# First norm through a diagonal product, early warm-up on a constant tile, and the first two chunks in pieces

## The reference

```python
def rms_norm(x, g):
    y = x * lax.rsqrt(jnp.mean(x * x, axis=-1, keepdims=True) + EPS)
    return y * g

h = rms_norm(x, norm1_g)
proj = h @ w_in          # split into the recurrent part, q, six k/v parts, gates, merge gates
...                      # recurrent unit, sparse attention, w_out, norm2, convolved FFN
...                      # second block: attention and gated MLP, layer norms, FFN
```

## Time and profile before

| what | value |
|---|---|
| median of 3 runs | 885.41 us |
| all runs | 885.78, 883.08, 885.41 us |
| time of the profiled execution | 883.73 us |
| its span in the trace | 882.0 us |
| mean granted TensorE clock | 0.994 |

### The profile page before, as it was taken

How to read it: one execution, slowest core, us unless ns; L and a number is a source line. 1 busy time by engine, 2 the same in 40 slices (tenths; PEclk the granted TensorE clock), 3 DMA queues, 4 the chain that set the end, 5 groups by cost and what they waited for, 6 DMA issues and landing times.

```text
span 882.0 us, 12692 instructions
## 1 busy us (share of the span) xinstructions
PE 853.0 (97%) x5239; PEld 745.5 (85%) x5239; DVE 576.9 (65%) x733; ACT 488.0 (55%) x713; POOL 37.6 (4%) x44
## 2 busy tenths in 40 slices
PE   6999999999999999999999999999989999999995
PEld 5899999888899998788888888877868788888884
DVE  4672487776765766598877777765765564555555
ACT  4463368777765544476656655435654554554542
POOL 0100200000000000100000000022110000000001
PEclk9999999999999999999999999999999999999999
DMA  6545524132334567245565555575325456456441
GB/s 251 187 145 206 189 84 171 46 138 93 118 132 144 177 229 265 94 171 189 188 199 184 191 192 190 172 239 186 107 74 216 137 189 231 149 187 222 160 143 48
DMA packets 22073, 146.31 MB, mean 166 GB/s; under 512 B 2432, under 2 KB 2688, under 8 KB 7552
## 3 DMA queue, kind: packets, MB, share of 16 engines
q1 hardware_dynamic: 20880, 140.27, 45.5%
q10 hardware_dynamic: 1136, 5.24, 1.7%
HBM read 144.45 MB, written 1.05 MB: 165 GB/s over the span
## 4 chain that ended last, share of the span: by engine, by line
PE 82%; DVE 7%; ACT 4%; issue 3%; DMA 2%; POOL 1%; ACTq 0%; SPq 0%; DVEq 0%; POOLq 0%
PE PS L1454 18%; PE PS L1455 9%; PE PS L1442 8%; PE PS L1444 7%; PE PS L1443 7%; PE PS L1464 7%; PE PS L1466 7%; PE PS L1465 7%; PE PS L1689 2%; DVE WL L897 2%; PE PS L1490 1%; DMA RAW<-in_w_stream 1%; PE PS L1546 1%; ACT WH L546 1%; DVE CG L1287 1%
## 5 line engine op out<-in xcount | busy, mean ns | idle before, releaser
L897 DVE TENSOR_TENSOR WL<-RAW,WH 128x2048 fp32r<-128x2048 f32 (+3 forms) x130 | 287.9, 2216 | 77.7 <-ACT WH L546 77.5
L546 ACT ACTIVATE WH<-RAW 128x2048 fp32r<-128x2048 f32 (+3 forms) x130 | 241.1, 1856 | 81.3 <-PE PS L1466 31.7
L1454 PE MATMUL PS<-CHL,WH 128*128 128x512 f32 x384 | 135.5, 397 | 0.5 <-DVE WL L897 0.3
L1454 PE MATMUL PS<-BHL,WH 128*128 128x512 f32 x352 | 125.4, 400 | 0.1
L1442 PE MATMUL PS<-BHL,WH 128*128 128x256 f32 (+2 forms) x424 | 120.4, 284 | 0.0
L1444 PE MATMUL PS<-BHL,WL 128*128 128x256 f32 (+2 forms) x424 | 119.5, 282 | 0.0
L1443 PE MATMUL PS<-BHL,WH 128*128 128x256 f32 (+2 forms) x424 | 119.5, 282 | 0.0
L1455 PE MATMUL PS<-CHL,WL 128*128 128x256 f32 x384 | 107.7, 281 | 0.0
L1276 DVE TENSOR_TENSOR HLS<-PS,HLS 128x512 f32<-128x512 f32 x46 | 31.8, 692 | 105.1 <-ACT HLS L819 104.3
L1455 PE MATMUL PS<-BHL,WL 128*128 128x256 f32 x352 | 99.0, 281 | 0.0
L1454 PEld LDWEIGHTS PS<-CHL,WH 128*128 128x128 f32 x384 | 72.1, 188 | 18.5 <-DVE WL L897 0.7
(11 more groups left out here) (266 smaller groups left out, 1420.4 us busy)
## 6 DMA issues: line engine op xcount, KB each, us to landing
RAW<-in_w_stream SPq DMA_DIRECT2D x109, 1024.0 KB, 4.9
RAW<-in_w_stream SPq DMA_DIRECT2D x12, 896.0 KB, 5.2
RAW<-in_w_stream SPq DMA_DIRECT2D x8, 768.0 KB, 4.2
WF<-in_w_stream SPq DMA_DIRECT2D x4, 784.0 KB, 4.3
WF<-in_w_stream SPq DMA_DIRECT2D x2, 1024.0 KB, 4.9
LN<-in_ln ACTq DMA_DIRECT2D x2, 1024.0 KB, 6.3
X<-in_x SPq DMA_DIRECT2D x2, 512.0 KB, 4.1
X<-in_x ACTq DMA_DIRECT2D x1, 1024.0 KB, 4.8
```

Source lines behind the costliest of these rows:

```text
L546: eng.activation(WH[:, c % NSLOT, 0:CHUNKS[c][2]], raw(c), ACT.Copy).then_inc(w_hi, 1)
L897: eng.tensor_tensor(WL[:, c % NSLOT, 0:CHUNKS[c][2]], raw(c), f32(WH[:, c % NSLOT, 0:CHUNKS[c][2]]), ALU.subtract).then_inc(w_lo, 1)
L1454: eng.matmul(PS[:, bank, :], wh, HL[:, k, :, :].rearrange("p a t -> p (a t)"), start=(k == 0), stop=False)
```

## The change

The first norm is no longer done on x. DVE multiplies the identity by the inverse roots of a tile, which gives a diagonal DG (128 x 128). TensorE multiplies x (stationary) by DG (moving): that transposes x and scales each token in one ordinary float32 product. The gains are now a column per channel group (G1, 128 x 8) and are applied when PSUM is read: ACT as the scale of its copy (`gained_hi`), DVE in a scalar_tensor_tensor (`gained_lo`), 256 columns at a time.

TensorE first multiplies a tile of ones by itself, 14 times 128 columns wide, written by a memset of DVE. The 8 products with the identity are gone.

The loads G1 and the identity part of CN are issued by ACT. The rest of CN and CV are issued by SP behind chunk 1. ACT's copies of identity and mask move to the first cmp chunk (chunk 4).

Chunk 0 is split in two halves on ACT and DVE, each followed by a pair of channel groups; chunk 1 is split whole, then pairs 2 and 3 follow. TensorE works chunks 0 and 1 by pairs of channel groups (two groups, both tiles), each as soon as it is ready, in place of tile by tile.

Some semaphores are merged: G2R counts on `x_again`, and LN1, OGR and GLN on `rows_in`, of which every reader waits for all three. The numbers computed are those of the reference.

```diff
@@ SP
-            eng.dma_start(G1R[:, :], A_g1.partition_broadcast(P)).then_inc(g1_in, 16)
-            eng.dma_start(CN[:, :], A_consts).then_inc(const_in, 16)
             for c in LOAD_ORDER:
-                if c == 1:
+                if c == 2:
+                    eng.dma_start(CN[:, P:NCONST], A_consts[:, P:NCONST]).then_inc(const_in, 16)
                     eng.dma_start(CV[:, :], A_cols).then_inc(col_in, 16)
@@ ACT
+            def gained_hi(kp):
+                eng.wait_ge(xt_done, kp + 1)
+                for k in (2 * kp, 2 * kp + 1):
+                    last = eng.activation(BH[:, k, :], PS[:, kp, 256 * (k % 2):256 * (k % 2) + TOK], ACT.Copy,
+                                          scale=G1[:, k:k + 1])
+                last.then_inc(xt_hi, 1)
+
+            eng.dma_start(G1[:, :], A_g1).then_inc(g1_in, 16)
+            eng.dma_start(CN[:, 0:P], A_consts[:, 0:P]).then_inc(g1_in, 16)
             for t in range(NT):
                 eng.wait_ge(x_in[t], 16)
                 eng.activation(XN[:, t, :], X0[:, t, :], ACT.Square, accum_out=ssx[:, t:t + 1]).then_inc(x_sq, 1)
-            evict_hi(BH, XT_BANKS[0], xt_done, xt_hi, kps=(0, 1))
-            split(0)
-            evict_hi(BH, XT_BANKS[0], xt_done, xt_hi, kps=(2, 3), first=2)
+            eng.wait_ge(g1_in, 32)
+            eng.wait_ge(raw_in[ARRIVAL[0][0]], 16)
+            for kp, ready in enumerate((w0_half, w_hi)):
+                part = slice(CHUNK // 2 * kp, CHUNK // 2 * kp + CHUNK // 2)
+                eng.activation(WH[:, 0, part], raw(0)[:, part], ACT.Copy).then_inc(ready, 1)
+                gained_hi(kp)
             split(1)
-            eng.wait_ge(const_in, 16)
-            eng.activation(IDR[:, :], ident, ACT.Copy)
-            eng.activation(MASKR[:, :], const("mask"), ACT.Copy).then_inc(masks_ready, 1)
+            gained_hi(2)
+            gained_hi(3)
             for c in range(NCH):
+                if c == AT["cmp", 0]:
+                    eng.wait_ge(const_in, 16)
+                    eng.activation(IDR[:, :], ident, ACT.Copy)
+                    eng.activation(MASKR[:, :], const("mask"), ACT.Copy).then_inc(masks_ready, 1)
@@ DVE
-            eng.wait_ge(g1_in, 16)
+            def gained_lo(kp):
+                eng.wait_ge(xt_hi, kp + 1)
+                for k in (2 * kp, 2 * kp + 1):
+                    last = eng.scalar_tensor_tensor(BL[:, k, :], PS[:, kp, 256 * (k % 2):256 * (k % 2) + TOK], G1[:, k:k + 1],
+                                                    f32(BH[:, k, :]), ALU.mult, ALU.subtract)
+                last.then_inc(xt_lo, 1)
+
+            eng.memset(WARM[:, :], 1.0).then_inc(warm_ready, 1)
+            eng.wait_ge(g1_in, 32)
             for t in range(NT):
                 eng.wait_ge(x_rstd, t + 1)
-                eng.scalar_tensor_tensor(XN[:, t, :], X0[:, t, :], rsx[:, t:t + 1], G1R[:, :], ALU.mult, ALU.mult)\
-                   .then_inc(xn_ready, 1)
-            evict_lo(BH, BL, XT_BANKS[0], xt_hi, xt_lo, kps=(0, 1))
-            split(0)
-            evict_lo(BH, BL, XT_BANKS[0], xt_hi, xt_lo, kps=(2, 3), first=2)
+                eng.tensor_scalar(DG[:, t, :], ident, rsx[:, t:t + 1], None, ALU.mult).then_inc(dg_ready, 1)
+            for kp, (ready, low) in enumerate(((w0_half, w0_lo), (w_hi, w_lo))):
+                part = slice(CHUNK // 2 * kp, CHUNK // 2 * kp + CHUNK // 2)
+                eng.wait_ge(ready, 1)
+                eng.tensor_tensor(WL[:, 0, part], raw(0)[:, part], f32(WH[:, 0, part]), ALU.subtract).then_inc(low, 1)
+                gained_lo(kp)
             split(1)
+            gained_lo(2)
+            gained_lo(3)
@@ TensorE, main(c)
-                    eng.wait_ge(xt_lo, (2, 4)[i > 0])
                     b = 4 + 2 * (i // 2)
-                    last = t_half(c, (b, b + 1), i, BH, BL)
+                    if i < 2:
+                        for kp in (2 * i, 2 * i + 1):
+                            eng.wait_ge(xt_lo, kp + 1)
+                            if kp == 1:
+                                eng.wait_ge(w_lo, 1)
+                            for t in range(NT):
+                                ks = [(k, 512 * (k % 4)) for k in (2 * kp, 2 * kp + 1)]
+                                last = t_part(PS[:, b + t, :], c, 512, ks, BH, BL, t, kp == 0, kp == 3)
+                                if kp == 3 and t == 0:
+                                    last.then_inc(tile0_done, 1)
+                    else:
+                        last = t_half(c, (b, b + 1), i, BH, BL)
@@ TensorE, start
-            eng.wait_ge(const_in, 16)
-            transposes(XN, XT_BANKS[0], xn_ready, xt_done)
-            for _ in range(8):
-                eng.matmul(PS[:, 4, 0:TOK], ident, XN[:, 0, 0:TOK], start=True, stop=True)
+            eng.wait_ge(warm_ready, 1)
+            for _ in range(14):
+                eng.matmul(PS[:, 4, 0:P], WARM[:, :], WARM[:, :], start=True, stop=True)
+            for t in range(NT):
+                eng.wait_ge(dg_ready, t + 1)
+                for kp in range(4):
+                    for kk in range(2):
+                        k = 2 * kp + kk
+                        last = eng.matmul(PS[:, kp, 256 * kk + P * t:256 * kk + P * t + P], X0[:, t, P * k:P * k + P],
+                                          DG[:, t, :], start=True, stop=True)
+                    if t == NT - 1:
+                        last.then_inc(xt_done, 1)
```

More of the change, by code:

```diff
@@ L302, in two_block_program @@
         XN = put("XN", [P, NT, DM], at=pr + 66560)
-        G1R = put("G1R", [P, DM], at=pr + 41984)
+        DG = put("DG", [P, NT, P], at=pr + 41984)
+        G1 = put("G1", [P, KD], at=pr + 43008)
+        WARM = put("WARM", [P, P], at=pr + 43072)
         KSQ = put("KSQ", [P, 2, 256], at=pr + 66560)
@@ L355, in two_block_program @@
             "w_hi", "w_lo", "chunk_done", "tile0_done", "ri_part", "y_gain", "x_again", "const_in", "g1_in"))
[L356 to L359, removed]
+        warm_ready, rows_in, w0_half, dg_ready, ln2_in, ws_in, out_done, act_own, dve_own = (sem(n) for n in (
+            "warm_ready", "rows_in", "w0_half", "dg_ready", "ln2_in", "ws_in", "out_done", "act_own", "dve_own"))
+        pool_own, x_sq, x_rstd, w0_lo, xt_done, xt_hi, xt_lo, k_sq, k_ss = (sem(n) for n in (
+            "pool_own", "x_sq", "x_rstd", "w0_lo", "xt_done", "xt_hi", "xt_lo", "k_sq", "k_ss"))
         k_rstd, kn_ready, kt_done, kt_copied, gk_ready, mb_act, mb_dve, gate_tanh = (sem(n) for n in (
@@ L711, in side @@
                         eng.wait_ge(qk_done, NU)
-                        eng.dma_start(G2R[:, :], A_g2.partition_broadcast(P)).then_inc(g2_in, 16)
+                        eng.dma_start(G2R[:, :], A_g2.partition_broadcast(P)).then_inc(x_again, 16)
                     if i >= 1:
@@ L735, in side @@
                 if kind == "dn" and i == N_UP // 2 - 1:
-                    for a, b, s in ((LN1, A_ln1, ln1_in), (OGR, A_og, og_in), (GLN, A_gln, gln_in)):
+                    for a, b in ((LN1, A_ln1), (OGR, A_og), (GLN, A_gln)):
                         if a is LN1:
@@ L1135, in side @@
                     if n == 0:
-                        eng.wait_ge(x_again, 16)
+                        eng.wait_ge(x_again, 32)
                     for t in range(NT):
@@ L1207, in side @@
                         ins.then_inc(z_ss, 1)
-                        eng.wait_ge(gln_in, 16)
+                        eng.wait_ge(rows_in, 48)
                         for t in range(NT):
@@ L1339, in layer_norm @@
                 y, gained = (X1, X3) if n == 0 else (X3, X1)
-                gains, gains_in = ((LN1, ln1_in), (LN2, ln2_in))[n]
+                gains, gains_in, landed = ((LN1, rows_in, 48), (LN2, ln2_in, 16))[n]
                 def gain(t):
@@ L1365, in layer_norm @@
                     if t == 0:
-                        eng.wait_ge(gains_in, 16)
+                        eng.wait_ge(gains_in, landed)
                         gain(0)
@@ L1643, in main @@
                 kind, i, _, is_split = CHUNKS[c]
-                if is_split:
+                if is_split and c:
                     eng.wait_ge(w_lo, SPLIT_NO[c] + 1)
+                elif is_split:
+                    eng.wait_ge(w0_lo, 1)
                 else:
@@ L1985 @@
         "consts": consts,
-        "g1": row("norm1_g"),
+        "g1": np.ascontiguousarray(a["norm1_g"].reshape(KD, P).T),
         "g2": row("norm2_g"),
```

5 lines of the change are left out of this document (2 added, 3 removed).

## The result

| what | before | changed |
|---|---|---|
| median of this comparison | 884.25 us | 875.79 us |
| its runs | 4, 881.75 to 885.78 | 4, 875.21 to 877.95 |
| profiled execution, its span, mean granted clock | 883.73, 882.0 us, 0.994 | 875.21, 873.5 us, 0.996 |
| chunk 0's first product in the profile | 16.63 us | 11.85 us |

The ratio is 0.9928, interval 0.9904 to 0.9951: faster by 6.4 us (4.3 to 8.5). The forecast was a gain of 4.7 and a median of 880.7, within 878.4 to 883.9.

The account below looks back on a forecast made before the run. The prediction took TensorE, 97% busy in a closed row of matmuls behind 16.6 us, as the bound. Starting that row 4.7 us earlier took 883.73 to 879.0, plus 1.7 for the median: 880.7 us, range 878.4 to 883.9.

Parts of the forecast that it names:

- The front: Kernel start up to chunk 0's first product: it would start at 11.9 us, not 16.63, 4.7 us earlier (4.0 to 5.3).
- W0: Load of chunk 0's weights at the start: would land at 8.6 us instead of 10.7, ends 8.3 to 9.1.
- W2: Chunk 2's load, behind chunk 0's low part: would land at 17.7 us, its chunk ready at 22.1, needed at 22.8.
- The rule on transposes: Skill page's FP32 transpose rule, applied to the 16 front products: 0.456 us each, 7.3 in all; earlier rows contradicted it.
- slow products: Rival at the front: products take 0.456 us each, chunk 0 starts at 14.4, gain 2.2, median 883.2; chance 0.10.
- its other condition: The slow products rival's alternative cause: TensorE's clock level has not risen by 7 us, so products take 0.456 us each.
- The row stayed closed: TensorE's matmuls behind chunk 0 would run without holes; two chunks' load and splitting take 9.3 us against 10.9 of products.
- What is won at 22 us arrives at the end: From chunk 1's end to the kernel's end: the whole 4.7 us won at the start would be kept.
- The rest, at nothing: Moved constant loads and copies, ACT's DMA issues, chunk 1 by pairs and merged waits would cost no time.
- the sum: Whole kernel: 883.73 less 4.7 gives 879.0; the median of three runs lies 1.7 above the profiled execution, so 880.7 us.
- Behind that no wait hangs on absolute time: Behind the first chunks, no wait would end at its old time and give the 4.7 us gain back.
- The range: Whole kernel's median: 878.4 to 883.9 us, from gains of 4.0 to 5.3, three runs' spread and slow products at 883.2.

Follow-up runs that it names:

- a_whole: The changed kernel with chunks 0 and 1 split whole and worked tile by tile as before the change: median 882.79 us, ratio to before 1.0015.
- b_warm: b_late_edits with the memset and 14 warm-up products put ahead of its transposes: median 881.56 us, ratio to before 0.9986.
- b_late_edits: The kernel before with only the merged waits and ACT's identity and mask copies moved to chunk 4: median 881.34 us, ratio to before 0.9987.
- b_rows_later: The kernel before with the LN1, OGR and GLN loads issued at in2 chunk 4: median 880.73 us, ratio to before 0.9981.

## Why the prediction was right and wrong

**The front was right, term by term.** DG of tile 0 was done at 7.17 (predicted 6.95) and the products began at 7.22 (7.1). The 32 product instructions took 3.84 us, 0.240 a product against the 0.25 taken from the earlier trace rows. W0 landed at 8.6, as worked out from the earlier trace rows (8.35 or 8.7; the 8.6 lies nearer the second). Chunk 0 started at 11.85 against 11.9, chunk 1 ended at 22.9 against 22.8, W2 landed at 17.7 as said. Two terms were low and covered: a pair of evictions took 0.84 on ACT (taken 0.66, from the plain 256-wide ones) and 0.87 on DVE (taken 0.76). The hand-overs were shorter by as much. The level rose at 14.5 us in the kernel before (its first clock record), not at 14.2. When it rises changes from execution to execution: the same 28 warm-up instructions took 5.59 us here, 6.18 in a_whole and 4.85 in b_warm.

**The rule on transposes.** The earlier trace rows have eight float32 transposes in 1.03 us at the full level, about 0.11 apart with the last one's drain taken off; the 32 new product instructions stand as far apart, two to a product. So an ordinary float32 product of 128 columns costs twice a transpose here. The Trainium skill, "TensorE: Matmul & The Clock Gate", "Terms", says of transpose mode that it is four times faster for FP32. Counted in time per operation, the trace of this case has two times and not four. It can't tell whether the transpose as such is faster, since products 32 columns wide come no closer than 0.11 us either (a row of the changed kernel):

```profile
102.78 3.65 PE L1603 MATMUL PS<-KCZ,QT 128*128 128x32 f32 x32
```

The rival built on four times ("slow products", 883.2) fell, as did its other condition, since the level had risen before the products.

**The row stayed closed.** "What is won at 22 us arrives at the end" held: held by 4.35 and 6.6 us, the changed kernel lost 4.5 and 6.5 in span x clock (from 869.9 to 874.4 and 876.3). Held by 2.2 it lost 3.3, a microsecond more, which no run explains. "The rest, at nothing" held too: b_late_edits is within 0.13% of before, and the merged waits have no row in the waits of the changed kernel.

**The step that failed is the sum.** It read: the profiled execution took 883.73; 883.73 - 4.7 = 879.0; the median of three lies 1.7 above it, so 880.7. Both numbers from which the 4.7 was taken stood high, by chance as far as the runs show.
- The median of three stood high. Over all 108 executions of the kernel before in these comparisons the median is 881.9, the mean 882.4, the standard deviation 1.6, from 880.0 to 886.3. Three shown at 883.08 to 885.78 were all from its upper third; three in a row from there come some 3 times in 100, and no run shows another reason.
- The profiled execution held two events that I took for fixed parts of the kernel: the RQK wait (1.4 us) and the low stretch at 656 us (1.6 us). The wait stood in the very trace I read. "Behind that no wait hangs on absolute time" wasn't false, since the wait costs an early and a late start the same; but whether it comes at all goes, by b_rows_later, with when one load lands.

With 881.9 in place of 885.4 the same 4.7 gives 877.2. The gain was a little small as well: 5.5 came. The 16 executions of the changed kernel have a median of 876.4 and a mean of 876.8.

**The gain.** Pooled, it is 5.5 us; in span x clock 875.74 - 869.86 = 5.9. The kernels with the rows loaded later differ by 874.8 - 869.3 = 5.5, at starts of 16.86 and 11.78: 5.1 us of start and 0.4 unexplained. So 4.8 of the 5.9 are the start. The rest can in part be an RQK wait that comes less often: moving the row loads is worth 0.9 in the kernel before (875.7 to 874.8) and 0.6 in the changed one (869.9 to 869.3), though 0.3 between them is within the noise. What makes the whole of this last microsecond is not shown. The low level near 105 us may be what makes the 5.5 smaller than the 5.9. So of the 8.5 us between the two profiles 4.8 were the change's front and most of the rest was chance. Of the front, the pieces bring 3.5 us of start and the full level for chunk 0, the warm-up 2.1 (with the diagonal there; by itself nothing). These overlap and don't add.

**The range** was built from the front's terms and three runs. It reached 2.3 us below the forecast, while the centre from which it was taken, 885.4, alone stood 3.5 too high.

**Still open.** Whether and why the RQK wait is rarer in the changed kernel than in its delayed copies; where the last microsecond of the gain comes from; what brings the low level near 105 us. What the diagonal brings apart from the moved loads was not tried.

## What to carry to other kernels

When a forecast is finer than the scatter of single executions, the first thing to price is the scatter: a wait or a low-clock stretch far from the change, seen in one profile, is not a constant of the kernel, and a median of three can stand 3 us beside the long-run one. Where TensorE's work is a closed row, shorten what stands before its first product, by working the first chunk in pieces, each handed on as it is done; that also shortens TensorE's pause, and behind a pause of 4.5 us the next two chunks took 2.5 us more, their first part at the low level. Bulk loads that nobody needs soon belong away from a load that is awaited: moving three row loads took 1.2 us in span x clock and most of its scatter off the kernel before.

## What was unexpected of the hardware

- POOL's 128 x 512 product took 1.29 us where no split ran and about 3.3 us when it began just behind one on DVE (2.55 against 4.63 us for two). It goes both ways: a split that began behind POOL's took 2.92 and not 2.29 us. One late load turned that into a stall of TensorE.
- TensorE's low level comes in stretches of 3.4 or 6.8 us, also where TensorE is busy throughout, and not in every execution of the same code. One costs 1.5 or 3.0 us, a quarter to a half of what this change brings.
- The first half of a 1 MB load, issued by itself ahead of the second, landed at 8.40 us, where the whole load of the changed kernel landed at 8.60.
